# Conv tiles in pairs of seven half products, q and k made and rotated by features, in a hybrid decoder block on one core

## The reference, cut to what matters

```
u    = rms_norm(x, norm_mix_pre_w)
proj = u @ w_in       # z 2048 | xbc 3072 | dt 32 | q 1024 | k 256 | v 256 | two gates of 1024
xbc  = silu(causal_dwconv(xbc, ssd_conv_w, ssd_conv_b))       # 4 taps along the tokens
q, k = apply_rope(q), apply_rope(k)                           # halves of 32 in each head of 64
y_ssd  = gated_group_rms_norm(ssd_chunked(...) + d * xs, z, ssd_norm_w) @ ssd_w_out
y_attn = sliding_window_sink_attention(q, k, v, sinks) @ attn_w_out       # window 128
x = x + rms_norm((sigmoid(gate_ssd) * y_ssd + sigmoid(gate_attn) * y_attn) @ w_mix_out, ...)
x = x + rms_norm(conv_ffn(rms_norm(x, ...)), ...)
```

## Time and profile before

| | us |
|---|---|
| median of 3 runs | 2081.97 (2081.32 to 2081.98) |
| span of the profiled execution | 2080.7 |
| TensorE busy | 2048.5 (98%) |
| VectorE busy | 1205.3 (58%) |
| ScalarE busy | 891.7 (43%) |
| GpSimd busy | 590.0 (28%) |

### The profile page before, as it was taken

How to read it: one execution, slowest core, us unless ns; L and a number is a source line. 1 busy time by engine, 2 the same in 40 slices (tenths; PEclk the granted TensorE clock), 3 DMA queues, 4 the chain that set the end, 5 groups by cost and what they waited for, 6 DMA issues and landing times. The chain is left out here.

```text
span 2080.7 us, 27724 instructions
## 1 busy us (share of the span) xinstructions
PE 2048.5 (98%) x9980; PEld 1682.0 (81%) x9980; DVE 1205.3 (58%) x1676; ACT 891.7 (43%) x1720; POOL 590.0 (28%) x573
## 2 busy tenths in 40 slices
PE   7999999999999999999999999999999999999997
PEld 7888889987777777777778888888888888888886
DVE  6855453226565576565634445569877787753523
ACT  5332222026666566665633223345444444444432
POOL 1000011146576676676500000024222222100000
PEclk9999999999999999999999999999999999999999
DMA  6222342324353444443454343322212221455453
GB/s 229 75 88 81 101 152 91 106 77 139 123 146 113 140 146 129 130 115 112 155 199 154 130 152 130 116 81 82 91 61 90 91 85 66 162 177 184 120 147 91
DMA packets 131254, 252.61 MB, mean 121 GB/s; under 512 B 25265, under 2 KB 70449, under 8 KB 131153
## 3 DMA queue, kind: packets, MB, share of 16 engines
q1 hardware_dynamic: 86304, 177.60, 26.7%
q0 software_dynamic: 14496, 52.17, 7.4%
q10 hardware_dynamic: 30352, 21.50, 3.2%
HBM read 189.63 MB, written 61.60 MB: 121 GB/s over the span
## 5 line engine op out<-in xcount | busy, mean ns | idle before, releaser
L158 PE MATMUL ps_zg<-u_hi,g_hi 128*128 128x512 f32 x448 | 184.2, 411 | 0.0
L160 PE MATMUL ps_zg<-u_hi,g_lo 128*128 128x512 f32 x448 | 175.7, 392 | 0.0
L159 PE MATMUL ps_zg<-u_lo,g_hi 128*128 128x512 f32 x448 | 174.8, 390 | 0.0
L2354 DVE TENSOR_TENSOR lt_d_lo<-lt_w_raw,lt_d_hi 128x640 fp32r<-128x640 f32 (+1 forms) x62 | 55.3, 891 | 133.6 <-ACT lt_d_hi L2053 133.5
L1924 POOL TENSOR_TENSOR lt_t_f<-lt_w_raw 128x512 f32<-128x512 f32 x21 | 29.1, 1385 | 261.8 <-DVE lt_t_lo L2282 260.3
L158 PE MATMUL ps_zg<-z_w,u_hi 128*128 128x512 f32 x256 | 102.8, 401 | 0.0
L1090 POOL TENSOR_TENSOR mx_seg<-mx_seg,mx_cbm 128x1024 f32<-128x1024 f32 x31 | 74.5, 2403 | 92.4 <-ACT mx_seg L1194 88.5
L160 PE MATMUL ps_zg<-z_w,u_lo 128*128 128x512 f32 x256 | 100.2, 391 | 0.0
L2053 ACT ACTIVATE lt_d_hi<-lt_w_raw 128x640 fp32r<-128x640 f32 (+1 forms) x62 | 49.1, 792 | 118.9 <-PE lt_ps L160 98.3
L159 PE MATMUL ps_zg<-z_w,u_hi 128*128 128x512 f32 x256 | 99.7, 389 | 0.0
L160 PEld LDWEIGHTS ps_zg<-u_hi,g_lo 128*128 128x128 f32 x448 | 84.0, 188 | 18.6
(11 more groups left out here) (455 smaller groups left out, 6258.5 us busy)
## 6 DMA issues: line engine op xcount, KB each, us to landing
lt_w_raw<-in_w_up SPq DMA_DIRECT2D x44, 512.0 KB, 4.3
work<-acs_s SPq DMA_DIRECT2D x32, 512.0 KB, 3.9
g_raw<-in_w_xbc SPq DMA_DIRECT2D x24, 512.0 KB, 3.3
lt_sig<-gate_s SPq DMA_DIRECT2D x24, 512.0 KB, 3.7
lt_w_raw<-in_w_down SPq DMA_DIRECT2D x32, 384.0 KB, 3.2
ff_s<-lt_fo SPq DMA_DIRECT2D x21, 512.0 KB, 4.7
tok_s<-work POOLq DMA_DIRECT2D x20, 512.0 KB, 3.8
lt_w_raw<-in_w_down SPq DMA_DIRECT2D x32, 320.0 KB, 3.0
```

The source lines that it names most:

```text
L158: pe.matmul(dst, s_hi, m_hi, start=first, stop=False)
L159: pe.matmul(dst, s_hi, m_lo, start=False, stop=False)
L160: return pe.matmul(dst, s_lo, m_hi, start=False, stop=last)
L2354: dve.tensor_tensor(down_w(m)[1][:, 0:n], w_raw[:, m % 2, 0:n], down_w(m)[0][:, 0:n].bitcast(F32), ALU.subtract).then_inc(dw_lo_done, 1)
```

## The change

- RC is 1 and only dt and v are made by tokens: `rows(t)` has 288 moving columns (VW = 32 + 256), once for each of the eight token tiles. v goes to `v_s`.
- The 24 conv tiles and the 10 feature tiles of q and k are 17 pairs, in the order `ORDER` ("c" is conv, "r" is rotated). Pair 0 is made of 8 half products of 12 matmuls, three of them between the rows of the first loop. Pairs 1 to 16 are made of 7. The sums of u (`s1` to `s4`) are made in the first loop on ACT, DVE and POOL, those of the weights (`t1` to `t4`) on POOL for each pair, the recombination (`u2`, `u3`, c22, c21, c12) on DVE. s3 takes the place of one quarter of u, which is spilled to `u_s` and read back at the end.
- The sine and cosine: POOL reduces the angles in 41 dependent operations, ACT makes sine and cosine repeated over the heads, PE transposes them (`turn_trig`, 16 transposes in pair 1), ACT copies them out. A pair of q or k tiles is rotated by features: ACT copies a tile out of PSUM, SP swaps its 32-partition halves by four DMAs, POOL multiplies by the sine, DVE by the cosine and adds, SP stores it in `q_s`.
- ACT, not DVE, copies the transposed conv tiles out; SP's queue, not POOL's, stores.
- At the end of `front` SP loads the second half of z once four products of pair 16 are done; it then loads step 0, does the swaps of pair 16, loads step 1, reads back u and stores pair 16.
- `mixers`: no rotation, no transposes of q and k, no copies of them; `q_t` and `k_t` are loaded (k in four places instead of two). SP's loads of step c + 2 wait for `scored` instead of `rotated`.

```diff
-RC = 4
+RC = 1
+VW = NH + NG * HD
+ORDER = (("c", 0), ("c", 1), ("r", 0), ("c", 8), ("r", 4), ("c", 10), ("c", 2), ("c", 3), ("r", 1), ("c", 4), ("c", 9),
+         ("r", 2), ("c", 5), ("c", 6), ("c", 7), ("c", 11), ("r", 3))
 # PE, front
-            for t in range(1, NT):
-                if t + 1 < NT:
-                    turn_x(t + 1)
-                rows(0, t)
-            tile(0, 0, True)
...
-            for c in range(1, RC):
-                for t in range(NT):
-                    rows(c, t)
+            for i in range(1, N_PAIRS):
+                a, b = 2 * i, 2 * i + 1
+                before = tiles[a - 2], tiles[a - 1]
+                op(i, 2)
...
+                product(bank(a, 0), b11(i), a11, True).then_inc(product_done, 1)
+                if i == 1:
+                    turn_trig(0)
...
+                product(bank(a, 1), (t3_hi, t3_lo), a21, True).then_inc(product_done, 1)
+                if i == 1:
+                    turn_trig(1)
+                    pe.wait_ge(sum_lo_done, 1)
+                op(i, 4)
+                slot_free(pe, b)
+                product(bank(b, 1), (t2_hi, t2_lo), (s2_hi, s2_lo), True).then_inc(product_done, 1)
+                if before[0].turns:
+                    turn(a - 2)
...
+                product(bank(b, 0), (t1_hi, t1_lo), (s1_hi, s1_lo), True).then_inc(product_done, 1)
...
+                product(bank(a, 0), b21(i), a12, False).then_inc(product_done, 1)
+                if before[1].turns:
+                    turn(a - 1)
+                pe.wait_ge(u3_ready, i)
+                op(i, 6)
+                product(bank(a, 1), (t4_hi, t4_lo), a22, False).then_inc(product_done, 1)
+                pe.wait_ge(c22_ready, i)
...
+                product(bank(b, 0), b22(i), (s4_hi, s4_lo), False).then_inc(product_done, 1)
+            def turn_trig(n):
+                pe.wait_ge(trig_ready, n + 1)
+                if n:
+                    pe.wait_ge(trig_out, n)
 # ACT, front
+            hi_b21(1)
+            act.wait_ge(cw_in, 16)
+            taken(0)
+            act.wait_ge(v_stored, 16)
+            act.wait_ge(s1_ready, TH)
+            act.activation(s1_hi[:], s1_f[:], ACT.Copy).then_inc(sum_hi_done, 1)
+            hi_t4(1)
...
+            act.activation(s4_hi[:], s4_f[:], ACT.Copy).then_inc(sum_hi_done, 1)
+            for i in range(1, LAST):
+                a, b = tiles[2 * i - 2], tiles[2 * i - 1]
+                hi_b22(i)
+                if a.conv:
+                    silu(a.n)
+                keep_p1(i)
+                taken(b.n)
+                if i == 1:
+                    trig(0)
+                    trig(1)
+                hi_t3(i + 1)
+                if a.turns:
+                    by_tokens(a.n)
+                if b.conv:
+                    silu(b.n)
 # DVE, front
+            low_sum(2, s1_lo, s1_f, s1_hi)
+            c12(0)
+            lo_t4(1)
+            low_sum(3, s4_lo, s4_f, s4_hi)
+            for i in range(1, LAST):
+                finish(2 * i - 2)
...
+                lo_b22(i)
...
+                lo_t3(i + 1)
+                finish(2 * i - 1)
+                u2_of(i)
+                u3_of(i)
+                c22(i)
 # PE, mixers
-                    pe.wait_ge(rotated, n + 1)
-                    for a in range(3):
-                        two = (carry.qr if opening else qr)[:, 2 * a:2 * a + 2].rearrange("p a d -> p (a d)")
-                        last = pe.transpose(ps_a[:, a * P:(a + 1) * P], two, ident[:])
-                    last.then_inc(qk_turned, 1)
```

More of the change, by code:

```diff
@@ new lines, in xc_free, with xt_free @@
+        def xc_free(eng, n):
+            if n < 2:
+                eng.wait_ge(rows_done, NT)
+                return
+            before = tiles[n - 2]
+            if not before.conv:
+                eng.wait_ge(q_stored[before.j], 16 * (before.q_n + 1))
+            if before.turns:
+                eng.wait_ge(turned, before.turn_n + 1)
+            if before.feats:
+                eng.wait_ge(f_stored[before.j], 16 * (before.feat_n + 1))
+        def xt_free(eng, n):
+            if n < 2:
+                eng.wait_ge(trig_turned, n + 1)
+                return
+            before = next((t for t in reversed(tiles[:n]) if t.j == n % 2 and (t.turns or not t.conv)), None)
+            if before.conv:
+                eng.wait_ge(t_stored[before.j], 16 * (before.tok_n + 1))
+            else:
+                eng.wait_ge(rot_done, before.rot_n + 1)
@@ new lines, in _ @@
+            table_turns(FAR)
+            table_turns(1.0, last=True)
+            for t in range(TH, NT):
+                sums(t)
+            weight_sum_3(1)
+            weight_sums(1)
+            for i in range(1, LAST):
+                turning = not tiles[2 * i - 2].conv
+                if turning:
+                    by_sine(2 * i - 2)
+                weight_sum_3(i + 1)
+                if turning:
+                    by_sine(2 * i - 1)
+                weight_sums(i + 1)
+            pool.wait_ge(carry.step_in[0], 16 * 8)
@@ L772, in _ @@
+            for k in range(4):
+                low_z(k)
+            c21(i)
+            for k in range(4, KT):
+                low_z(k)
+            c12(i)
             dve.wait_ge(carry.g_hi_done, 1)
@@ L831, in tile, with product @@
-            def tile(i, j, first, turns=True):
-                f = 2 * i + j
-                pe.wait_ge(lo_done, f + 1)
-                if not first:
-                    pe.wait_ge(conv_done, f - 1)
-                half(i, j, 0)
-                half(i, j, 1).then_inc(product_done, 1)
-                if turns and not (first and j == 0):
-                    turn(f - 1, 1 - j, first and j == 1)
+            def product(dst, w, block, fresh):
+                for k in range(KH):
+                    last = matmul3(pe, dst, w[0][:, k], w[1][:, k], block[0][:, k], block[1][:, k],
+                                   fresh and k == 0, k == KH - 1, not fresh)
+                return last
@@ new lines, in op, with turn @@
+            def op(i, n):
+                pe.wait_ge(op_lo_done, OPS * (i - 1) + n)
+            def turn(n):
+                t = tiles[n]
+                pe.wait_ge(silu_done, t.conv_n + 1)
+                if t.turn_n:
+                    pe.wait_ge(t_out, t.turn_n)
+                else:
+                    pe.wait_ge(trig_out, 2)
+                for k in range(NT):
+                    last = pe.transpose(ps_t[:, k], xc[:, t.j, k * P:(k + 1) * P], ident[:])
+                last.then_inc(turned, 1)
@@ L855, in _ @@
             turn_x(0)
[L856 removed]
+            rows(0, range(0, KH))
             turn_x(1)
[L858 removed]
+            rows(0, range(KH, KT))
             for t in range(1, NT):
@@ L1016, in group @@
                     if not (last and c >= NT - 2):
-                        for sem in (diag_done, xd_ready, rotated, pv_done):
+                        for sem in (diag_done, xd_ready, scored, pv_done):
                             sp.wait_ge(sem, NT * g + c + 1)
```

1114 lines of the change are left out of this document (682 added, 432 removed).

## The result

After the change the kernel takes 2124.45 us, median of 4 runs (2122.18 to 2126.71), against 2081.97 before: ratio 1.0203, 95% interval 1.0188 to 1.0217. It is 2% slower where 2071 was forecast. The profiled execution has a span of 2121.5 us, granted clock 0.979.

What follows compares the result with a forecast made beforehand. TensorE's instructions were taken to be the time (98% busy). `front` came out at 453.0 us against 452.2 (+0.8), the mixers saved 11.8: 2080.7 + 0.8 - 11.8 = 2069.7, median 2071 us, range 2046 to 2088.

Steps and rivals of the forecast that it cites:

- the mixers: Mixer stage: removing three transposes of 0.38 us in each of 32 steps saves 11.8 us, lower bound 4.
- (d): Pairs behind the four inner rotated ones: TensorE waits for u3, 4 us each, 17 us in all, bounds 4 and 24.
- (f): TensorE's clock in `front`: two long waits each cost 1.5 us of slowed clock, 3 us, bounds 0 and 6.
- (a): Start of `front`: the first loop's chain and DVE-POOL interference put pair 0's end at 77.8 us, bounds 75 and 81.
- (b): Pair 1: TensorE waits 13.7 us at the second `turn_trig` for ACT's copy, bounds 11 and 16; pair ends at 114.1.
- (c): Pairs 2 to 16 without waits: matmuls, turned tiles and the table's small products take 302.9 us, to 417.0.
- the term of 1.5: Pairs 2 to 16: the table's small products, unchanged, take 1.5 us.
- (e): End of `front`: copy, swap, sine, add, store and barrier behind pair 16's last product take about 16 us, bounds 12 and 21.
- Rival 3: TensorE's clock falls in every gap, those of 4 us too; four more falls at up to 2.9 us: 2083; chance 0.09.
- rival 4: The mixers do not give the transposes' time back because something else ends last there: 2082 us; chance 0.07.
- Rival 2: Steady pairs: the chain is late beyond 0.8 us to spare; 2 us longer costs 21 over 15 pairs: 2092; chance 0.12.
- Rival 1: Waits in `front` are covered because engines run further ahead than ordered: 2031 us; chance 0.12.

Runs made afterwards that it cites:

- e4: Kernel after the change, with the sine product moved from GpSimd to VectorE behind the cosine product: 2108.7 us.
- e5: Kernel after the change, with the order around pair 1 changed on ScalarE, VectorE and TensorE so the angle tables are copied earlier: 2111.8 us.
- e1: Kernel after the change, with the rotation of all ten q and k tiles left out, tables still made: 2055.8 us.
- e10: Kernel after the change, with 184 unused matmuls put ahead of the u3 waits in the four rotated pairs: 2115.5 us.
- e2: Kernel after the change, with only VectorE's order changed in the four turns that rotate, most other work going ahead of the rotations: 2086.1 us.
- e8: Kernel after the change, with GpSimd's subtraction held at changes of group until VectorE has the z weights' low parts: 2117.3 us.
- e6: Kernel after the change, with e5's order, both rotations behind u3, the dt table in three parts and a reordered tail: 2088.0 us.

## Why the prediction was wrong

The sum against 2071: start +2, pair 1 +1, the u3 waits +29, what pairs 2 to 16 took beyond them +6 (9 us, nearly all of it the clock, against my 3), the tail +3, the mixers +10, 51 of the 53 us. The misses that matter are one step of (d), the size of (f) and the mixers.

(a) The end of pair 0 came at 79.9, inside my bounds (75 to 81), 2.1 past my value: the scalings of x took 1.28 to 1.81 us, 1.46 in the mean, for 1.29, and the last loop turns were later. I had set the Trainium skill's whole-instruction rule against a mean of 1.03 us and let the mean decide. By the records at e4 the rule holds here; a mean over mixed cases can't refute it. I should have looked at single operations in that row's timeline.

(b) Right in place and size: 11.7 us at the second `turn_trig`, on ScalarE (13.7 forecast, bounds 11 and 16). The mechanism, order alone, fits e5, which took the wait away by reordering. The product behind it ran at half rate, the wait's share of (f).

(c) Right: 303.1 us without the rotation (e1) for 302.9. (By the numbers that it names, the term of 1.5 should have been 1.9.)

(d) The step that failed. Its mechanism was the right one, u3 queued behind tile b's rotation, but I gave it 4 us each where 8.6 to 14.3 were measured. Four terms in it were too small. Tile a's swap lands 5.7, 3.4, 3.5 and 7.0 us after the start of the four pairs, not 2.8: the four issues on SP stand 0.63 us apart, and in the first of these pairs one transfer took 4.5 us to land, in the last all four took 5.4 to 5.8, where 2.3 is usual (why, no run shows). Tile a's rotation takes 4.7 to 5.8 us from landing to c12, not 3.8, by exclusion (e4: 15.8 us). c12 and with it tile b's copy and swap come after this, and tile b's rotation meets GpSimd again, so exclusion is paid twice. And the dt table, which I counted at 1 us and at i = 5 alone, lies between at i = 3 as well, there with 8.8 us, one of its operations behind a sine for 2.2. From the pair's start u3 was due at 17.1 by my chain and came at 28.0 at i = 3; at i = 9 and 12, where no dt table stands, it came at 22.3 and 25.9.

(e) 18.6 us for 16, within the bounds, with the same exclusion in it: the cosine and add of tile 32 took 3.4 and 3.2 us beside the two sines.

(f) I counted two waits as long enough to slow the clock and took 1.5 us each. All six were long enough (the second turn's, the four for u3, the barrier's); the four in the rotated pairs cost 8 (e10), 2.0 each. Most of this follows from (d): with waits of 4 us there would have been the two, and at most part of the four. Rival 3 supposed it of gaps of 4 us too: in e2, matmuls 0.43 us apart followed a wait of 2.95 us, and none followed one of 3.21, so such a gap can cost it and need not. The Trainium skill (TensorE: Matmul & The Clock Gate, "Why this matters for your kernels") has an idle gap between bursts of matmuls drop the clock to half, and the long waits agree.

The mixers gave 1.4 us and not 11.8 (rival 4 in its outcome). Three terms: a step got 0.28 us shorter and not 0.38, since ps_d pays 0.10 more once it is first (3 us in all); the pair of steps at the three changes of group got 1.1, 1.6 and 1.6 us longer where it should have got shorter, GpSimd's subtraction lying on the z splits (e8); the first step took 18.4 us for 16.2, part of it slow from the barrier's wait (15.9 in e1, where that wait is 3.05). Term (f) had no place for a wait's price in the stage that follows.

Rival 2 was wrong: a turned pair takes 20.86 us, at 0.227 a matmul. (Its price did not follow either: 2 us less the 0.8 to spare is 1.2, and 15 times that 18, not 21.) Rival 1 was wrong: no wait it named was covered, and even without any rotation the kernel takes 2055.8, not 2031.

What would have caught it: chain (d) was drawn with each operation at the duration it has alone, and the engine's order was followed only from tile b on. Drawing the whole turn, from the previous turn's last transfer, with GpSimd's and VectorE's operations laid end to end where they meet, is the way to see it.

## What to carry to other kernels

When work is added to an engine that has room on average, write out its queue in the turn that gets it and find what stands behind it that another engine waits for: here the same operations cost 46 us of waits in one order and 15 in another. Two products that VectorE and GpSimd could share in parallel were not parallel here, both operands of each lying in SBUF; it was better to let the engine that is twice as fast take both (e4), and to hold back a large operation on the other (e8). The waits of about ten microseconds on TensorE cost two more each behind them (e10); price that also in the stage that follows.

## What the hardware showed that I had not expected

- VectorE and GpSimd exclude each other both ways and by whole operations: a sine of 2.34 us on GpSimd became 3.4 beside a cosine of 1.23; an operation of 0.42 us on VectorE became 2.59 beside a sine; an add of 1.23 became 2.2 beside a weight sum.
- Four transfers between blocks of 32 partitions cost SP 2.4 us of issue; each lands 2.4 us after its issue in the median, but after 5.4 to 5.8 in one of the pairs of after, and after 6.1 to 7.9 where the mixers' first loads are queued ahead (e6).
- Three transposes taken out of TensorE did not give back all they took: the next instruction became 0.10 us longer, of 0.38.
- Making GpSimd wait gave 6 to 7 us (e8).
